# A weight stream placed between the steps of a serial chain by a table, and split in half chunks

## The chip, the cores and the metric

The kernel runs on one core of a Trainium2 chip. The metric is the device time of one execution in microseconds (us), the median of the timed runs. The engines are TensorE (PE), VectorE (DVE), ScalarE (ACT), GpSimd (POOL) and SyncE (SP), each with its own queue of instructions that it works through in order. They wait for each other with semaphores only.

## The reference, cut to what matters

Two decoder layers are computed for 256 prompt tokens and 8 sample tokens together, T = 264 columns with D_MODEL = 2048. All in float32:

```python
# per layer
h = x @ w_in                                   # 2048 x 19024, columns shared out among five branches
# A gated delta rule (chunked, triangular solve)    B sparse attention: indexer, top-k, gather, softmax
# C retention (chunkwise recurrent)                 D RG-LRU: conv, gates, linear scan
# E cross-attention into 256 memory tokens (w_mem_kv)
merged = sum(sigmoid(gate_b) * (y_b @ w_branch[b]) for b in branches)
out = merged @ w_out                           # 2048 x 2048
x = layer_norm(ALPHA * x + out)
...
s = jnp.einsum('bqhd,bsd->bqhs', qi_blk, ki_all).astype(jnp.float32)      # indexer
score = jnp.einsum('bqhs,bqh->bqs', jax.nn.relu(s), w_blk.astype(jnp.float32))
_, idx = lax.top_k(score, ksel)                # 256 of 2049 keys for each sample, 64 of 256 in the prompt
...
m = jnp.eye(c) + jnp.where(strict, beta[..., :, None] * kk * decay, 0.0)  # delta rule
sol = lax.linalg.triangular_solve(m, rhs, left_side=True, lower=True, unit_diagonal=True)
```

## The kernel before, in words

Two kinds of work share the engines. The **weight stream** is dense: each layer has 174 chunks of 128 output columns and the whole contraction (2048 rows, KC = 16 K steps). For each chunk SP loads 1 MB into one of two `ring` buffers (L520). ACT rounds it to the high part of a split in fp32r (L1022), DVE subtracts to get the low part (L1267), each into one of two `wsplit` buffers, and PE does three matmuls for each K step (high x high, high x low, low x high, L564 to L566) with the activations `xsplit`, into a bank of `mb`. The 8 chunks of w_mem_kv are not split (L554, L557). ACT evacuates a chunk (`stored`, or the sigmoid of a gate). A chunk of a gate has four more matmuls behind it, the branch projection (L575), each two instructions in float32, and DVE multiplies and adds into `merged` (L1295, L1297, L1298).

The **chain** is everything else: a long series of small steps, each of which needs the one before. PE does a few small matmuls or transposes into `bb`, DVE or ACT works on the result, PE goes on. In order of the program: memory attention (`attend(0)`, `sample_attend(0)`), small gates, the lightning indexer over 8 page groups (L738, L743, L747), three convolutions (L1531), norms, the triangular inverse (two tiles of six levels, L843, L847, L848), the delta rule's output, its state steps for samples (`samples_step`, L881, L889), retention with its own, RG-LRU, rotations, copies of rows to the outputs, prompt indexer, sparse attention, gather and `sample_attend(1)`. The top-k of the samples is 32 rounds of four DVE instructions on a row of 2049 scores (`topk`, L1313 to L1316), strewn over the chain from the inverse on. The state tiles, the keys and the values for samples come by POOL's DMA queue.

The order of all work is written out by hand. In the code of each engine `stream(n)` stands between chain steps and issues that engine's part of the next n chunks, whole chunks only. On ACT and DVE `ahead()` and `stream` also issue the split of the coming chunk (`split_to`). PE runs its `stream` behind the chain matmul whose answer it will wait for. Behind the last chain step `stream(None)` issues what is left. A branch's gates may only be streamed once its output is done.

The numbers behind the letters: a K step is three matmuls, a branch step one float32 matmul, a layer has 2784 K steps and 320 branch steps. The lines of the small functions named here are below.

## Time and profile before

| | |
|---|---|
| median of three runs | 3554.73 us (3553.57 to 3561.67) |
| profiled execution, first to last instruction | 3562.9 us |
| TensorE busy | 3125.1 us, 88% |
| VectorE busy | 2040.6 us, 57% |
| ScalarE busy | 940.3 us, 26% |
| mean granted TensorE clock | 0.913 |
| DMA | 485.89 MB, mean 136 GB/s |

The spans of matmuls overlap, since they are pipelined, so a sum of their lengths is more than PE's busy time. Idle time counts only on the engine that the others wait for. The granted clock is 1.00 at 2.4 GHz and 0.50 at 1.2 GHz; a mean between them says how long either held.

### The profile page before, as it was taken

What the parts mean: (1) busy time and instruction counts of PE and PEld (TensorE: products, weight loads), DVE (VectorE), ACT (ScalarE), POOL (GpSimd) and SP (SyncE); (2) the same over time, 40 slices, a digit from 0 to 9 for tenths busy, and PEclk for the clock granted to TensorE, in tenths of its full rate; (3) what the DMA queues carried; (4) which work ended last, traced back from release to release, by engine and by line L of the source; (5) the groups of instructions that cost most, each with busy time, mean ns of one, the idle gap of its engine ahead of it and who ended that gap; (6) DMA issues with size and microseconds to landing.
All of it is one profiled execution on the core that took longest, in us unless ns stands there. A gap on an engine that the chain in (4) does not pass through costs nothing. (4 is left out here: it accounts for less than half of the span.)

```text
span 3562.9 us, 50279 instructions
## 1 busy us (share of the span) xinstructions
PE 3125.1 (88%) x21476; PEld 2907.0 (82%) x21476; DVE 2040.6 (57%) x2274; ACT 940.3 (26%) x969; POOL 186.2 (5%) x206
## 2 busy tenths in 40 slices
PE   6998887898888999999779988888978879999995
PEld 5888787887777898999778887788878778989995
DVE  2153267769868776344413532766798697653444
ACT  2232132212133232223313222322121422322232
POOL 0000000000000002100000000000000000031000
PEclk9988898998889999999989888999898999999998
DMA  5664343353544556665356632433535445675651
GB/s 154 166 173 129 101 121 83 104 142 107 148 116 107 161 148 192 169 175 157 83 139 174 189 103 87 121 103 108 138 101 143 128 126 139 163 197 164 177 157 60
DMA packets 825220, 485.89 MB, mean 136 GB/s; under 512 B 20548, under 2 KB 807108, under 8 KB 823746
## 3 DMA queue, kind: packets, MB, share of 16 engines
q1 hardware_dynamic: 803760, 409.93, 43.3%
q0 software_dynamic: 19936, 66.89, 6.1%
q10 hardware_dynamic: 1296, 5.80, 0.4%
q8 instruction: 172, 2.82, 0.3%
q14 instruction: 56, 0.46, 0.0%
HBM read 466.22 MB, written 16.47 MB: 135 GB/s over the span
## 5 line engine op out<-in xcount | busy, mean ns | idle before, releaser
L564 PE MATMUL mb<-xsplit,wsplit 128*128 128x264 f32 (+1 forms) x5312 | 1615.1, 304 | 164.4 <-DVE wsplit L1267 150.9
L565 PE MATMUL mb<-xsplit,wsplit 128*128 128x264 f32 (+1 forms) x5312 | 1569.1, 295 | 0.0
L566 PE MATMUL mb<-xsplit,wsplit 128*128 128x264 f32 (+1 forms) x5312 | 1564.8, 295 | 0.0
L564 PEld LDWEIGHTS mb<-xsplit,wsplit 128*128 128x128 f32 (+1 forms) x5312 | 1066.5, 201 | 215.0 <-DVE wsplit L1267 168.4
L565 PEld LDWEIGHTS mb<-xsplit,wsplit 128*128 128x128 f32 (+1 forms) x5312 | 1065.6, 201 | 4.3
L566 PEld LDWEIGHTS mb<-xsplit,wsplit 128*128 128x128 f32 (+1 forms) x5312 | 1057.1, 199 | 1.1
L1267 DVE TENSOR_TENSOR wsplit<-ring,wsplit 128x2048 fp32r<-128x2048 f32 x332 | 753.1, 2269 | 338.2 <-ACT wsplit L1022 324.8
L1022 ACT ACTIVATE wsplit<-ring 128x2048 fp32r<-128x2048 f32 x332 | 627.8, 1891 | 165.6 <-PE mb L566 109.7
L1049 ACT ACTIVATE gbuf<-mb 128x264 f32<-128x264 f32 x160 | 62.6, 391 | 1024.2 <-PE mb L566 967.3
L575 PE MATMUL mb<-work,bring 128*128 128x264 f32 x1280 | 310.6, 385 | 0.0
L1297 DVE TENSOR_TENSOR gbuf<-gbuf,mb 128x264 f32<-128x264 f32 x128 | 54.8, 428 | 422.6 <-PE mb L575 420.3
L1063 ACT ACTIVATE work<-mb 128x264 f32<-128x264 f32 x136 | 52.9, 389 | 810.8 <-PE mb L566 810.8
L575 PEld LDWEIGHTS mb<-work,bring 128*128 128x128 f32 x1280 | 231.3, 189 | 31.6
L1313 DVE MAX8 m<-memkv 8x8 f32<-8x2049 f32 x64 | 145.7, 2277 | 0.1
L1314 DVE FIND_INDEX8 i<-m,memkv 8x8 uint32<-8x2049 f32 x64 | 145.6, 2275 | 0.0
L1315 DVE MATCH_REPLACE8 memkv<-m,memkv 8x2049 f32<-8x2049 f32 x64 | 145.1, 2267 | 0.0
L1489 DVE SCALAR_TENSOR_TENSOR work<-bb,scm 128x1024 f32<-128x1024 f32 x16 | 19.6, 1225 | 163.5 <-PE bb L743 163.5
L675 PEld LDWEIGHTS bb<-small,work 128*128 128x128 f32 x512 | 72.2, 227 | 11.5 <-DMA work<-in_cache_mem_v_dram 10.9
L675 PE MATMUL bb<-small,work 128*128 128x1 f32 x512 | 71.6, 274 | 10.6 <-DMA work<-in_cache_mem_v_dram 10.6
L889 PE MATMUL bb<-work 8*128 8x512 f32 x64 | 44.2, 823 | 31.6 <-DVE work L1650 31.6
L847 PE MATMUL bb<-work 128*128 128x128 f32 x192 | 47.9, 338 | 16.5 <-ACT work L1174 16.5
L747 PEld LDWEIGHTS bb<-tab,work 128*128 128x128 f32 x256 | 31.1, 199 | 34.3 <-DVE work L1489 34.3
(392 smaller groups left out, 2437.5 us busy)
## 6 DMA issues: line engine op xcount, KB each, us to landing
ring<-in_w_in_dram SPq DMA_DIRECT2D x296, 1024.0 KB, 5.8
bring<-in_w_branch_dram SPq DMA_DIRECT2D x160, 256.0 KB, 3.2
ring<-in_w_out_dram SPq DMA_DIRECT2D x32, 1024.0 KB, 6.0
ring<-in_w_mem_kv_dram SPq DMA_DIRECT2D x16, 1024.0 KB, 5.5
work<-in_cache_mem_k_dram POOLq DMA_DIRECT2D x16, 512.0 KB, 4.1
work<-in_cache_mem_v_dram POOLq DMA_DIRECT2D x16, 512.0 KB, 4.1
work<-in_mem_prompt_dram ACTq DMA_DIRECT2D x2, 2048.0 KB, 12.2
work<-in_state_gdn_dram POOLq DMA_DIRECT2D x8, 512.0 KB, 5.1
```

Of the source, the lines that this page charges most:

```text
L564: pe.matmul(bank[0:n, 0:T], wh, ah, start=first, stop=False)
L565: pe.matmul(bank[0:n, 0:T], wh, al, start=False, stop=False)
L566: mm = pe.matmul(bank[0:n, 0:T], wl, ah, start=False, stop=last)
L575: mm = pe.matmul(mb[:, (g + 1) % 4, 0:T], bring[:, j % 2, q, :], y[:, q, :], start=(q == 0), stop=(q == CPS - 1))
L675: mm = pe.matmul(bb[:, 0, j:j + 1], kvb[:, b % 2, t, h * P:(h + 1) * P], pts[:, 32 * t + j:32 * t + j + 1], start=(t == 0), stop=(t == 1))
L1022: act.activation(hi(wsplit[:, s % 2, 0, :, 0:n]), ring[:, j % NRING, :, 0:n], ACT.Copy)\
L1049: act.activation(gbuf[:, :], src[:, 0:T], ACT.Sigmoid).then_inc(sem.gate_act, 1)
L1267: dve.tensor_tensor(hi(wsplit[:, s % 2, 1, :, 0:n]), ring[:, j % NRING, :, 0:n], wsplit[:, s % 2, 0, :, 0:n], ALU.subtract).then_inc(sem.l ...
L1297: v(dve.tensor_tensor(gbuf[:, :], gbuf[:, :], proj, ALU.mult))
L1313: v(dve.max(m8[:, :], srow))
L1314: v(dve.max_index(i8[:, :], m8[:, :], srow))
L1315: v(dve.match_replace(srow, m8[:, :], srow, TAKEN))
```

## The change

The stream is issued in steps instead of chunks. `STEP` lists all K steps and branch steps of a layer in order. The table `PACE` gives each chain step's name and how many steps PE runs behind it (`fill`). ACT and DVE have `before(name)` and `upto(pos)`: they issue all splits and evacuations that are due at a position of the stream. Chunks, their order and the chain's order stay. The load, the high part and the low part of a chunk are made in two halves of 8 K steps, with four half buffers in `ring` and in `wsplit`, so the bytes held are the same. A buffer of `wsplit` comes free after half a chunk (`half_mm`). DVE's part of a split is due four steps behind ACT's. Top-k rounds are cut by stream work at a third and two thirds of the fill they are named after. Splitting `merged` for w_out begins during the last gate (`merged_hi`, `merged_lo`). A semaphore without a reader, `lc_ok`, is gone.

```diff
-NRING = 2
+NRING = 4
...
+HALF = KC // 2
+for _i, (_k, _, _) in enumerate(CHUNKS):
+    START.append(len(STEP))
+    STEP.extend((_i, q) for q in range(KC + CPS * (_k == "gate")))
+def half_done(s):
+    return START[SPLIT[s // 2]] + HALF * (1 + s % 2)
+def hi_due(s):
+    i = SPLIT[s // 2]
+    read = done(i - 2) if i >= 2 and CHUNKS[i - 2][0] == "mem" else 0
+    return max(read, half_done(s - 4) if s >= 4 else 0)
+def lo_due(s):
+    return hi_due(s) + 4 * (s >= 4)
...
+PACE = """
...
+    gc 13  tail0 26  tail1 27  tail2 25  conv 24  ss1 19  norm1 6  ss2 25  tok0 12  kk 6  invT0 5  invA0 12  y00 3
...
-        ring = sb("ring", [P, NRING, KC, P])
-        wsplit = sb("wsplit", [P, 2, 2, KC, P])
+        ring = sb("ring", [P, NRING, HALF, P])
+        wsplit = sb("wsplit", [P, 4, 2, HALF, P])
...
+                        for half in range(2):
+                            r = 2 * i + half
+                            if i >= 2:
+                                if CHUNKS[i - 2][0] == "mem":
+                                    sp.wait_ge(sem.chunk_mm, products(i - 2))
+                                else:
+                                    sp.wait_ge(sem.lo_ok, 2 * SPLIT_N[i - 2] + half + 1)
+                            sp.dma_start(ring[:, r % NRING, :, 0:n], w[:, half * HALF:(half + 1) * HALF, c0:c0 + n])\
+                                .then_inc(w_landed[r % NRING], 16)
...
+                    def stream(n):
+                        for i, q in STEP[at[0]:at[0] + n]:
+                            if q < KC:
+                                weight_step(i, q)
+                            else:
+                                branch_step(i, q - KC)
+                        at[0] += n
+                    def fill(name):
+                        stream(FILL[name])
...
-                            stream(2)
+                            fill(f"lg{n}{t}")
...
+                    def upto(pos):
+                        while True:
+                            s, i = nxt_half[0], nxt_chunk[0]
+                            a = hi_due(s) if s < 2 * len(SPLIT) else pos + 1
+                            b = (START[i] if CHUNKS[i][0] == "out" else START[i] + KC) if i < len(CHUNKS) else pos + 1
+                            if min(a, b) > pos:
+                                return
+                            if a <= b:
+                                split_half(s)
+                                nxt_half[0] += 1
+                            else:
+                                evacuate(i)
+                                nxt_chunk[0] += 1
...
+                    def merged_hi(q):
+                        act.wait_ge(sem.merged_ok, LAST * KC + 4 * q + 4)
...
                             v(dve.max(m8[:, :], srow))
+                            upto(AT[name] + FILL[name] // 3)
                             v(dve.max_index(i8[:, :], m8[:, :], srow))
+                            upto(AT[name] + 2 * FILL[name] // 3)
                             v(dve.match_replace(srow, m8[:, :], srow, TAKEN))
                             v(dve.tensor_copy(picked[:, 8 * r:8 * r + 8], i8[:, :]))
+                            upto(AT[name] + FILL[name])
```

Three places show how instructions move. First DVE at the start of the delta rule's sample states: `COPY work<-bb 128x32` takes up PE's product of keys and queries, L1313 to L1316 are a top-k round, L1267 a split, L1295 a gate's finish. Before:

```order
L1625 COPY work<-bb 128x32 [waits qk_mm]
L1626 COPY work<-bb 8x512 [waits v_chain]
L1267 TENSOR_TENSOR wsplit<-ring,wsplit 128x2048 [waits hi_ok]
L1313 MAX m<-memkv 8x8
L1314 MAX_INDEX i<-m,memkv 8x8 [waits v_chain]
L1315 MATCH_REPLACE memkv<-m,memkv 8x2049 [waits v_chain]
L1316 COPY scm<-i 8x8 [waits v_chain]
L1295 TENSOR_TENSOR merged<-gbuf,mb 128x264 [waits chunk_mm,gate_act,v_chain]
```

In the changed kernel (L1389 to L1394 is the round, L1328 half a split, L1351 the gate's finish):

```order
L1701 COPY work<-bb 128x32 [waits qk_mm,v_chain]
L1702 COPY work<-bb 8x512 [waits v_chain]
L1389 MAX m<-memkv 8x8
L1391 MAX_INDEX i<-m,memkv 8x8 [waits v_chain]
L1328 TENSOR_TENSOR wsplit<-ring,wsplit 128x1024 [waits hi_ok,v_chain]
L1393 MATCH_REPLACE memkv<-m,memkv 8x2049
L1394 COPY scm<-i 8x8 [waits v_chain]
L1328 TENSOR_TENSOR wsplit<-ring,wsplit 128x1024 [waits hi_ok,v_chain]
L1351 TENSOR_TENSOR merged<-gbuf,mb 128x264 [waits chunk_mm,gate_act]
```

The split stood ahead of the round as one piece; its work is now two halves inside and behind the round.

Second DVE at the end of the RG-LRU, where L1727 is the product with the gate path and L1730 the copy that PE waits for. Before, from the second of two rounds on:

```order
L1313 MAX m<-memkv 8x8 [waits v_chain]
L1314 MAX_INDEX i<-m,memkv 8x8 [waits v_chain]
L1315 MATCH_REPLACE memkv<-m,memkv 8x2049 [waits v_chain]
L1316 COPY scm<-i 8x8 [waits v_chain]
L1297 TENSOR_TENSOR gbuf<-gbuf,mb 128x264 [waits chunk_mm,gate_act,v_chain]
L1298 TENSOR_TENSOR merged<-merged,gbuf 128x264 [waits v_chain]
L1267 TENSOR_TENSOR wsplit<-ring,wsplit 128x2048 [waits hi_ok]
L1297 TENSOR_TENSOR gbuf<-gbuf,mb 128x264 [waits chunk_mm,gate_act]
L1298 TENSOR_TENSOR merged<-merged,gbuf 128x264 [waits v_chain]
L1727 TENSOR_TENSOR work<-work 128x1056 [waits stored,lru_o]
L1730 COPY stg<-bb 9x512 [waits tail_out,h_mm,v_chain]
```

After, from the end of the first round on (L1795 and L1799 are that product and that copy):

```order
L1393 MATCH_REPLACE memkv<-m,memkv 8x2049
L1394 COPY scm<-i 8x8 [waits v_chain]
L1328 TENSOR_TENSOR wsplit<-ring,wsplit 128x1024 [waits hi_ok,v_chain]
L1328 TENSOR_TENSOR wsplit<-ring,wsplit 128x1024 [waits hi_ok]
L1353 TENSOR_TENSOR gbuf<-gbuf,mb 128x264 [waits chunk_mm,gate_act]
L1354 TENSOR_TENSOR merged<-merged,gbuf 128x264 [waits v_chain]
L1389 MAX m<-memkv 8x8
L1391 MAX_INDEX i<-m,memkv 8x8 [waits v_chain]
L1393 MATCH_REPLACE memkv<-m,memkv 8x2049 [waits v_chain]
L1394 COPY scm<-i 8x8 [waits v_chain]
L1795 TENSOR_TENSOR work<-work 128x1056 [waits stored,lru_o,v_chain]
L1799 COPY stg<-bb 9x512 [waits tail_out,h_mm,v_chain]
```

The splits and gates that stood behind the second round now all stand inside and behind the first, and the second is bare.

Third PE in the triangular inverse, between the first level's products (L847, L848) and the next level (L843). Before:

```order
L848 MATMUL bb<-work 128x128
L843 MATMUL bb<-work 128x128 [waits lvl_bt]
L843 MATMUL bb<-work 128x128 x3
L847 MATMUL bb<-work 128x128 [waits y_ok]
L848 MATMUL bb<-work 128x128
L847 MATMUL bb<-work 128x128
```

After, at the first level (L921 is the level's first product, L606 to L608 a K step, L625 a branch step, L926 and L927 the level's other products):

```order
L921 MATMUL bb<-work 128x128 [waits lvl_bt]
L921 MATMUL bb<-work 128x128 x3
L625 MATMUL mb<-work,bring 128x264 x2
L606 MATMUL mb<-xsplit,wsplit 128x264 [waits lo_ok,stored]
L607 MATMUL mb<-xsplit,wsplit 128x264
L608 MATMUL mb<-xsplit,wsplit 128x264
L926 MATMUL bb<-work 128x128 [waits y_ok]
L927 MATMUL bb<-work 128x128
```

Where no stream work stood there are now two branch steps and a K step at the wait for `y_ok`, and the table puts eight more behind the level's last product.

## Rows read from the trace of the kernel before

**Rows 1.** The cores view, and the engines' busy shares from the page.
```profile
core 0: 3562.9 us, clock 0.913
...
PE 3125.1 (88%) x21476; PEld 2907.0 (82%) x21476; DVE 2040.6 (57%) x2274; ACT 940.3 (26%) x969; POOL 186.2 (5%) x206
```

**Rows 2.** Windows of layer 1's chain, one of layer 2's; columns in the first line.
```profile
core 0: us, PE busy (x) PEld busy (x) DVE busy (x) ACT busy (x) POOL busy (x), PEclk, DMA share, GB/s
145.00:344.80 199.80, 181.26 (x1243) 168.34 (x1242) 92.94 (x103) 62.13 (x75) 15.43 (x21) 0.86 0.60 168
344.80:476.70 131.90, 113.66 (x680) 99.68 (x679) 34.06 (x36) 30.35 (x29) 8.05 (x7) 0.83 0.31 90
476.70:567.70 91.00, 74.05 (x551) 71.10 (x549) 68.99 (x109) 32.85 (x31) 3.61 (x7) 0.94 0.51 133
567.70:753.20 185.50, 164.54 (x1153) 156.73 (x1154) 120.51 (x124) 38.51 (x41) 3.14 (x4) 0.93 0.38 100
753.20:1022.20 269.00, 227.15 (x1414) 202.52 (x1412) 232.53 (x216) 56.42 (x52) 14.69 (x17) 0.84 0.48 129
1022.20:1261.80 239.60, 204.54 (x1414) 191.33 (x1413) 184.10 (x221) 74.96 (x77) 7.02 (x13) 0.94 0.48 130
1261.80:1477.10 215.30, 209.13 (x1462) 193.19 (x1460) 124.22 (x153) 63.26 (x71) 41.17 (x32) 0.96 0.65 180
1477.10:1745.50 268.40, 263.16 (x2002) 256.71 (x2001) 116.46 (x106) 79.10 (x62) 0.00 (x0) 0.99 0.59 157
1799.80:3235.00 1435.20, 1274.81 (x8627) 1178.81 (x8628) 871.64 (x974) 370.41 (x390) 92.84 (x101) 0.90 0.50 136
850.00:900.00 50.00, 36.47 (x230) 33.55 (x229) 49.24 (x38) 9.97 (x9) 0.00 (x0) 0.84 0.26 67
```

**Rows 3.** Windows with the stream alone: gates, then w_out.
```profile
1500.00:1550.00 50.00, 50.00 (x369) 48.16 (x368) 22.99 (x24) 15.34 (x14) 0.00 (x0) 1.00 0.65 174
1655.00:1745.00 90.00, 90.00 (x745) 90.00 (x745) 40.28 (x30) 26.89 (x14) 0.00 (x0) 1.00 0.56 152
```

**Rows 4.** Lines of the whole run: count, busy us, mean ns, idle before.
```profile
L1313 DVE MAX8 m<-memkv 8x8 f32<-8x2049 f32 x64 | 145.7, 2277 | 0.1
L1315 DVE MATCH_REPLACE8 memkv<-m,memkv 8x2049 f32<-8x2049 f32 x64 | 145.1, 2267 | 0.0
L1297 DVE TENSOR_TENSOR gbuf<-gbuf,mb 128x264 f32<-128x264 f32 x128 | 54.8, 428 | 422.6 <-PE mb L575 420.3 <-ACT gbuf L1049 1.5
```

**Rows 5.** Waits of the whole run: us in total, times, longest us.
```profile
PE mb L564 <- DVE wsplit L1267: 150.9, 54, 36.4
...
PE bb L747 <- DVE work L1489: 21.1, 16, 1.3
```

**Rows 6.** Lines: VectorE in 753.2 to 1022.2, then ScalarE in the whole run.
```profile
L1267 DVE TENSOR_TENSOR wsplit<-ring,wsplit 128x2048 fp32r<-128x2048 f32 x23 | 52.6, 2286 | 0.3
...
L1647 DVE TENSOR_TENSOR work<-work,tab 128x1024 f32<-128x1024 f32 x4 | 4.9, 1225 | 0.1
...
L1129 ACT ACTIVATE work<-bb 128x1024 f32<-128x1024 f32 x16 | 16.4, 1024 | 63.1 <-PE bb L738 63.1
```

**Rows 7.** DMA issues of the whole run: KB each, median us to landing.
```profile
ring<-in_w_in_dram SPq DMA_DIRECT2D x296, 1024.0 KB, 5.8
...
work<-in_cache_mem_k_dram POOLq DMA_DIRECT2D x16, 512.0 KB, 4.1
```

**Rows 8.** Timeline at the start of layer 2: start us, length us.
```profile
1788.76 11.56 SPq L520 DMA_DIRECT2D ring<-in_w_in_dram  x3
...
1795.55 1.91 ACT L1022 ACTIVATE wsplit<-ring 128x2048 fp32r<-128x2048 f32 x1 [5.43 <-DMA ring<-in_w_in_dram]
1798.83 1.91 ACT L1022 ACTIVATE wsplit<-ring 128x2048 fp32r<-128x2048 f32 x1 [1.37 <-DMA ring<-in_w_in_dram]
...
1797.49 2.29 DVE L1267 TENSOR_TENSOR wsplit<-ring,wsplit 128x2048 fp32r<-128x2048 f32 x1 [18.53 <-ACT wsplit L1022]
...
1799.84 0.59 PE L564 MATMUL mb<-xsplit,wsplit 128*128 128x264 f32 x1 [36.35 <-DVE wsplit L1267]
```

More of the change, by code:

```diff
@@ L132, in kv_count @@
+"""
+FILL, AT = {}, {}
+for _name, _n in zip(PACE.split()[::2], PACE.split()[1::2]):
+    AT[_name] = sum(FILL.values())
+    FILL[_name] = int(_n)
 def kv_count(n, i):
@@ L717, in _ @@
                     mm.then_inc(sem.ki_mm, 1)
-                    stream(1)
+                    fill("ki")
                     for c in range(CPS):
@@ L731, in _ @@
                     mm.then_inc(sem.new_mm, 1)
-                    stream(1)
+                    fill("new")
                     for j in range(8):
@@ L772, in tail @@
                         mm.then_inc(sem.tails, 1)
+                        fill(f"tail{i}")
                     def ones_sum(n, src):
@@ L1270, in _, with split_half @@
-                    at_chunk = [0]
-                    def ahead():
-                        split_to(at_chunk[0] + 1)
-                    def stream(n=1):
-                        for i in islice(chunks, n):
-                            (kind, x, m), g = CHUNKS[i], FIRST_RESULT[i]
-                            if kind == "gate" and x == LAST and m < 4:
+                    nxt_half, nxt_chunk = [0], [0]
+                    def split_half(s):
+                        i = SPLIT[s // 2]
+                        r = 2 * i + s % 2
+                        n = COL_NARROW[CHUNKS[i][2]][1] if CHUNKS[i][0] == "narrow" else P
+                        dve.wait_ge(sem.hi_ok, s + 1)
+                        dve.tensor_tensor(hi(wsplit[:, s % 4, 1, :, 0:n]), ring[:, r % NRING, :, 0:n],
+                                          wsplit[:, s % 4, 0, :, 0:n], ALU.subtract).then_inc(sem.lo_ok, 1)
@@ L1738, in _ @@
                     for j in range(7):
+                        before(f"row{j}")
                         dve.wait_ge(sem.rows_mm, 3 + j)
-                        ahead()
                         if j and j not in (4,):
```

635 lines of the change are left out of this document (314 added, 321 removed).

## The prediction

> **What bounds the kernel now.** I read span, clock and busy shares first [rows 1]: one program of 3562.9 us, about 8 us above the 3554.73 us median of the timed runs. TensorE (PE) is what the rest serves, since the weight stream runs through it from end to end. So I cut the span into stretches of layer 1 and read busy time and granted clock in each [rows 2]. The cuts are the starts of chain stages: 145.0 memory attention, 344.8 indexer, 476.7 convolutions and norms, 567.7 triangular inverse and delta rule, 753.2 sample states and retention, 1022.2 RG-LRU and row copies, 1261.8 sparse attention, 1477.1 stream alone until 1745.5. Layer 2 (from 1799.8) shows the same picture: 160.4 us idle and clock 0.90 in its chain part.
>
> A stretch loses PE time in two ways. Its idle time is its length less PE's busy time. Its clock loss is busy time times (1 less the granted clock), since the two levels are 2.4 and 1.2 GHz. In order of the stretches (idle + clock, us): 18.5+25.4, 18.2+19.3, 17.0+4.4, 21.0+11.5, 41.9+36.3, 35.1+12.3, 6.2+8.4, 5.2+2.6. That is 163 idle and 120 clock, 283 us of 1600.5.
>
> Third, where the stream runs dense, what does it cost? 745 recorded matmuls fill 90.0 us at full clock [rows 3], 0.121 us each, so a K step of three costs 0.36 us. In the stretch of gates alone 369 matmuls take 50 us, 56 to a gate: 7.6 us a gate, of which 5.8 are its 16 K steps and 1.8 its four branch steps, 0.44 each.
>
> Fourth, is VectorE (DVE) a second bound? It is busy 232.5 of 269.0 us in the stretch from 753.2, and 49.2 of 50.0 us in 850 to 900, where PE falls to 36.5 [rows 2]. A top-k round is three passes of 2.27 to 2.28 us, 6.8 us [rows 4], and a split is 2.29 [rows 6]. There the chain waits for DVE, not for PE. Last, the waits [rows 5]: the split is PE's largest releaser (150.9 us, 36.4 of it at a layer's start), and the others are many short ones, as the indexer's 16 waits of at most 1.3 us.
>
> **The change part by part.**
>
> *The stream spread over the waits.* Nothing is computed less. PE now runs whole chunks (5.8 us, a gate 7.6) at some waits and none at others, as the third block of order rows shows: no weight matmul between two levels of the inverse. After it every wait gets its own number of steps. I counted steps in both programs between the same chain steps. Per stretch, after less before (K steps, branch steps): +6/0, +1/0, +10/0, -29/-4, +110/+12, -6/+12, -77/-20, -15/0. They sum to nothing. At 0.36 and 0.44 us these are +2.2, +0.4, +3.6, -12.2, +44.9, +3.2, -36.6, -5.4 us. The full-clock floor of PE is the stretch less its loss plus this: 158.1, 94.8, 73.2, 140.8, 235.7, 195.4, 164.1, 255.2 us.
>
> *DVE's load moves with it.* The 110 steps taken into the stretch from 753.2 bring 6.9 more chunks at 2.29 = 15.7 us of splits [rows 6], and three more gate finishes, each one operation of 0.43 in the first branch's gates, 1.3 us [rows 4]. So stream goes to the place where DVE is fullest, away from 1261.8, where it has 124 of 215 us.
>
> *Splits in halves.* A DVE operation on 1024 columns from SBUF takes 1225 ns, one on 2048 columns 2286 in the same stretch [rows 4, 6]. Two halves cost 2450, so 0.16 us more per chunk, on DVE 332 x 0.16 = 54 us in all. It lies beside PE except where DVE leads: 479 steps or 30 chunks from 753.2, 4.8 us. ScalarE (ACT) has 1.91 us for a whole chunk [rows 8], and 1.02 for 1024 columns out of PSUM [rows 6]; if the half costs 1.0 to 1.1, two cost 0.1 to 0.3 more, hidden since ACT is busy at most 75 of 240 us in a stretch. DVE needs in the stretch from 753.2: 232.5+15.7+1.3+4.8 = 254.3 us. At the 98% that DVE reaches in 850 to 900 this is 259 us, at its present 86% it is 294. That is above PE's 235.7: DVE sets this stretch. In the stretch from 1022.2 (6 K steps fewer, three gates of two such operations more, 23.5 chunks in halves) it is 184.1-0.9+2.6+3.8 = 189.6 against PE's 195.4, in the one from 476.7 it is 72.1 against 73.2: neither hides the other.
>
> *Loads in halves, four buffers.* The same bytes are in flight. A 1024 KB load lands in 5.8 us, 512 KB in 4.1 [rows 7]. At a layer's start [rows 8] the load is issued at 1788.76, ACT starts at 1795.55, DVE at 1797.49, PE at 1799.84. With halves the landing comes 1.7 us earlier (5.8-4.1), ACT's part is 0.8 to 0.9 shorter and DVE's 1.1: 3.6 us, and about 4.5 if the first landing there gains more, since it took 6.8. I take 4.5, twice: 9 us. A buffer comes free every 2.9 us in the dense part, and each has 11.6 us for landing, both splits and its matmuls, so the loads hold.
>
> *The tail of the last gates.* The split of merged is started before the last gate is done. It is inside the 5.2 us of idle time of the last stretch; its end is counted below.
>
> *What stays of the losses.* No row shows a wait with a fill made for it. The lower end is that nothing stays: the floors, with 259 in place of 235.7, give 1341 us a layer, 259.5 saved, and 3562.9-519-9 = 3035. The upper end is that all stays as it is: with DVE at its present share the stretches from 753.2, 476.7 and 1022.2 grow with its work by 25.2, 4.1 and 7.2 us, the others change by their moved steps (-51.6), so 15.1 us a layer are saved and it is 3524. I take the middle, half of either loss: the waits that now get a fill were bare or half covered, but the clock falls also in stretches with hardly a gap, and top-k rounds of 6.8 us stand against fills of 15 to 17 steps (5.4 to 6.1). Stretches: 180.1, 113.5, 83.9, 157.1, 275 (DVE at 93%, between its two shares), 219.1, 171.4, 259.1: 1459.2 us, 141.3 saved a layer. In all 3562.9-282.6-9 = 3271 us as a profiled execution, 3263 beside the median.
>
> *Where the new order costs.* At the end of the RG-LRU (second block of order rows) the first of two top-k rounds is now cut up by all splits of a 71-step fill, and the second follows bare, before the copy that PE waits for. PE's fill is 55 K and 16 branch steps, 26.8 us. DVE has 10 halves (12.3), four gate finishes (3.4), two rounds (13.7) and 1.3 for the product before the copy: 30.7. PE waits some 4 us there per layer. Behind that copy PE has the rotations queued, and POOL its two stores. It is part of the half that stays.
>
> *The clock.* In the indexer PE's waits for DVE are 1.3 us at most [rows 5], and yet the granted clock is 0.83 with PE busy 113.7 of 131.9 us; from 476.7 to 567.7, with almost the same idle time in fewer us, it is 0.94 [rows 2]. The Trainium skill (TensorE: Matmul & The Clock Gate, "HAM oscillation — how this bites in real kernels") has it that long PE idle gaps bring the clock down, and that a kernel without them stays warm. By that rule all clock loss would go and the time would be some 120 us lower than my sum; the trace of the indexer does not agree, and so half of it stays.
>
> **The rivals.**
>
> *The clock stays as low.* The chain's narrow matmuls are all still there, and the indexer's row speaks for it. Then half of the clock loss outside the stretch that DVE sets, 42 us a layer, is not gained: 3263+84 = 3347 us.
>
> *Nearly everything is recovered.* The stretch 1500 to 1550 shows PE at 50.00 of 50.00 and clock 1.00 with the stream alone. If the fills reach that and a fifth of the loss stays, 3035+0.2x489 less 8 = 3125 us. Against it stand the top-k rounds above.
>
> *DVE is the bound all over.* Its share stays at today's in each stretch, and the spread only shifts PE's waits: the upper end, 3516 beside the median.
>
> *Half loads pay their fixed part one after another.* From [rows 7] 2x4.1-5.8 = 2.4 us. A chunk would take 8.2 us to load against 5.8 in the 16 chunks of w_out and 7.6 in 21 gates: 38+13 = 51 us a layer, 3263+102 = 3365. Against it: two whole loads in a row were split 3.3 us apart [rows 8], so loads overlap. The Trainium skill (DMA: Bandwidth & Descriptors, "Anatomy of one DMA — SWDGE (gpsimd) path") gives a fixed part of about 2.0 us per DMA, close to these 2.4; the rule speaks against the change only if nothing overlaps.
>
> *Slower: the top-k rounds get in the chain's way.* After the change a round is cut at a third and at two thirds of a fill and ends only when the splits due within that fill are done, which wait for PE's position. DVE can no longer run ahead of PE, and the chain's next DVE operation, with PE behind it, comes late. There are 32 rounds a layer. If three in four cost their 6.8 us on the path, 24x6.8 = 163 us a layer are given back, and it is 3263+326 = 3589 us. It decides from 21 rounds on (146 us). For it: the block at the end of the RG-LRU. Against it: most fills are about as long as DVE's work beside them.
>
> **How the numbers follow.** The forecast, half of the losses gone, 3265 us: 0.45, own range 3190 to 3330. Clock as low: 0.19. Nearly everything: 0.16. Half loads in a row: 0.05. DVE bound all over: 0.08. Slower: 0.07. The range of 8 in 10 is 3140 to 3420: it leaves out DVE all over, the slower case, and the tip of the low one. 0.3%, or 11 us, is what a measurement of this kernel tells from no change. Faster takes the first four and three quarters of DVE all over, since that end is itself uncertain by more than 11 us: 0.91. Same 0.02, slower 0.07.
>
> **What would show it right or wrong.** PE's busy share rises from 88% to 92 to 94%, and the mean granted clock from 0.913 to about 0.95. The stretch of sample states and retention stays near 270 us with DVE above 90% busy, the one of sparse attention falls from 215 to about 171, the indexer's from 132 to about 113. 664 splits of about 1.2 us stand on DVE and of 1.0 to 1.1 on ACT. The first matmul of layer 2 comes 4 to 5 us sooner after the first load is issued. Wrong would be: a clock below 0.92 with idle time halved (the first rival), ring loads above 6 us with ACT waiting for them in the dense part (the fourth), or PE waits for DVE behind top-k passes that sum to more than now (the last). The forecast falls if the stretch from 753.2 takes more than 300 us, or if sum of idle time in the chain part stays above 120 us a layer.

## The result, and the profile after

The changed kernel takes 3137.06 us, the median of four runs (3134.06 to 3142.06), against 3555.2 us (3553.57 to 3561.67) for the kernel before: ratio 0.8821, 95% interval 0.8809 to 0.8834. The direction was right. The forecast of 3265 us was 128 us too slow, and the time lies 3 us below the low end of the range. The case that came true is the second rival, nearly everything is recovered (3125 us), which had a chance of 0.16.

The cores view and the page's busy shares of the kernel after answer to [rows 1]. PE's busy time fell by 199 us although it issues the same 21476 matmuls; the clock losses summed below (120 us a layer before, 22 after) account for it:

```profile
core 0: 3135.3 us, clock 0.973
```

```profile
PE 2926.4 (93%) x21476; PEld 2747.5 (88%) x21476; DVE 2072.8 (66%) x2606; ACT 1005.7 (32%) x1303; POOL 170.1 (5%) x206
```

The windows view, cut at the same chain steps as in [rows 2], in the same order, with layer 2 as the last row:

```profile
core 0: us, PE busy (x) PEld busy (x) DVE busy (x) ACT busy (x) POOL busy (x), PEclk, DMA share, GB/s
138.20:304.00 165.80, 162.01 (x1265) 151.95 (x1265) 95.70 (x121) 67.51 (x99) 15.42 (x21) 1.00 0.72 207
304.00:395.30 91.30, 91.30 (x683) 83.41 (x682) 34.68 (x45) 28.93 (x34) 6.30 (x7) 1.00 0.47 134
395.30:477.80 82.50, 74.58 (x581) 72.09 (x579) 70.81 (x120) 35.70 (x45) 3.75 (x7) 0.98 0.54 149
477.80:624.00 146.20, 142.81 (x1098) 136.92 (x1099) 121.00 (x138) 39.16 (x52) 3.13 (x4) 1.00 0.44 122
624.00:889.40 265.40, 243.70 (x1729) 225.34 (x1728) 249.00 (x255) 80.48 (x97) 14.68 (x17) 0.95 0.56 156
889.40:1103.50 214.10, 199.09 (x1417) 187.31 (x1416) 188.92 (x262) 76.71 (x97) 7.05 (x13) 0.97 0.53 148
1103.50:1267.80 164.30, 163.99 (x1174) 150.44 (x1172) 105.26 (x143) 54.91 (x77) 34.71 (x32) 1.00 0.70 194
1267.80:1528.60 260.80, 258.33 (x1974) 252.01 (x1975) 121.69 (x143) 85.42 (x97) 0.00 (x0) 0.99 0.57 158
1578.00:2809.00 1231.00, 1176.60 (x8606) 1099.36 (x8606) 884.41 (x1104) 398.68 (x522) 84.88 (x101) 0.98 0.57 160
```

A stretch's length less PE's busy time, the two numbers behind the range, is its idle time; the clock stands behind POOL's numbers. The indexer's row is the plainest: 131.9 us with PE busy 113.66 at clock 0.83 [rows 2] has become 91.3 us, PE busy all of it, at 1.00. In sum layer 1's chain and stream take 1390.4 us, 210 less than before. Of the 163 us of idle time a layer 55 are left, of the 120 us of clock loss 22 (busy time times 1 less the clock, summed over the eight rows). The largest part of the one and more than half of the other, 21.7 and 12.2 us, are in the one row from 624.0, where DVE is busy 249.0 of 265.4 us.

The waits view of the kernel after (us in total, times, longest) answers to [rows 5]. The wait for the split is 59 us smaller, and 46 of its 91.5 us are the starts of the two layers (32.6 at the second, the longest; 13.5 by the same view of the first 304 us). The 21.1 us of the indexer's sixteen waits have no row any more. L778, the wait behind the end of the RG-LRU, is the largest inside the chain:

```profile
PE mb L606 <- DVE wsplit L1328: 91.5, 30, 32.6
...
PE bb L778 <- DVE stg L1799: 17.7, 2, 8.8
...
PE mb L606 <- DVE work L1618: 9.4, 2, 4.7
PE bb L970 <- DVE work L1726: 7.3, 6, 1.8
```

The lines of the split, by form (count, busy us, mean ns), answer to [rows 6]:

```profile
L1328 DVE TENSOR_TENSOR wsplit<-ring,wsplit 128x1024 fp32r<-128x1024 f32 x656 | 794.8, 1222 | 651.0 <-ACT wsplit L1108 641.5 <-issue 3.3
...
L1108 ACT ACTIVATE wsplit<-ring 128x1024 fp32r<-128x1024 f32 x656 | 692.4, 1058 | 1593.3 <-PE mb L608 1451.2 <-DMA ring<-in_w_in_dram 102.3 <-issue 39.0
```

And the timeline at the start of layer 2 answers to [rows 8]. From the load's issue to PE's first matmul it is now 7.07 us, 4.0 less than the 11.08 before. ACT starts on the first two half loads 1.81 us apart:

```profile
1573.10 7.55 SPq L561 DMA_DIRECT2D ring<-in_w_in_dram  x5
1577.80 1.06 ACT L1108 ACTIVATE wsplit<-ring 128x1024 fp32r<-128x1024 f32 x1 [3.44 <-DMA ring<-in_w_in_dram]
1578.89 1.23 DVE L1328 TENSOR_TENSOR wsplit<-ring,wsplit 128x1024 fp32r<-128x1024 f32 x1 [15.89 <-ACT wsplit L1108]
1579.61 1.06 ACT L1108 ACTIVATE wsplit<-ring 128x1024 fp32r<-128x1024 f32 x1 [0.75 <-DMA ring<-in_w_in_dram]
...
1580.17 0.59 PE L606 MATMUL mb<-xsplit,wsplit 128*128 128x264 f32 x1 [32.65 <-DVE wsplit L1328]
```

### The profile page after: what moved, and what is told of

Read it like the earlier page. It is cut to its first block and busy times, and to the rows that moved or that the text cites. A ratio compares the mean times of both kernels' runs of the same rounds, so it can differ in the third digit from the quotient of the medians.

```text
span 3135.3 us, 52446 instructions
## 1 busy us (share of the span) xinstructions
PE 2926.4 (93%) x21476; PEld 2747.5 (88%) x21476; DVE 2072.8 (66%) x2606; ACT 1005.7 (32%) x1303; POOL 170.1 (5%) x206
## 5 line engine op out<-in xcount | busy, mean ns | idle before, releaser
L606 PE MATMUL mb<-xsplit,wsplit 128*128 128x264 f32 (+1 forms) x5312 | 1589.6, 299 | 110.2 <-DVE wsplit L1328 91.5
L607 PE MATMUL mb<-xsplit,wsplit 128*128 128x264 f32 (+1 forms) x5312 | 1518.3, 286 | 0.0
L608 PE MATMUL mb<-xsplit,wsplit 128*128 128x264 f32 (+1 forms) x5312 | 1516.8, 286 | 0.0
L1328 DVE TENSOR_TENSOR wsplit<-ring,wsplit 128x1024 fp32r<-128x1024 f32 (+2 forms) x664 | 798.7, 1213 | 661.6 <-ACT wsplit L1108 651.9
L1108 ACT ACTIVATE wsplit<-ring 128x1024 fp32r<-128x1024 f32 (+2 forms) x664 | 696.2, 1051 | 1608.0 <-PE mb L608 1458.3
L606 PEld LDWEIGHTS mb<-xsplit,wsplit 128*128 128x128 f32 (+1 forms) x5312 | 1008.8, 190 | 169.3 <-DVE wsplit L1328 74.9
L607 PEld LDWEIGHTS mb<-xsplit,wsplit 128*128 128x128 f32 (+1 forms) x5312 | 1009.6, 190 | 10.5 <-issue 3.8
L608 PEld LDWEIGHTS mb<-xsplit,wsplit 128*128 128x128 f32 (+1 forms) x5312 | 1004.7, 189 | 1.1
L625 PE MATMUL mb<-work,bring 128*128 128x264 f32 x1280 | 318.7, 390 | 0.0
L625 PEld LDWEIGHTS mb<-work,bring 128*128 128x128 f32 x1280 | 232.9, 192 | 33.4 <-issue 1.5
L1389 DVE MAX8 m<-memkv 8x8 f32<-8x2049 f32 x64 | 145.6, 2275 | 0.0
L744 PE MATMUL bb<-small,work 128*128 128x1 f32 x512 | 58.9, 245 | 0.0
L1354 DVE TENSOR_TENSOR merged<-merged,gbuf 128x264 f32<-128x264 f32 x128 | 55.4, 433 | 4.4
L595 PE MATMUL mb<-ring,work 128*128 128x128 f32 x512 | 57.8, 275 | 0.0
L595 PEld LDWEIGHTS mb<-ring,work 128*128 128x128 f32 x512 | 57.6, 192 | 0.1
L592 PE MATMUL mb<-work,ring 128*128 128x256 f32 x256 | 55.6, 379 | 0.0
L592 PEld LDWEIGHTS mb<-work,ring 128*128 128x128 f32 x256 | 48.5, 190 | 6.5
## 6 DMA issues: line engine op xcount, KB each, us to landing
work<-in_mem_prompt_dram ACTq DMA_DIRECT2D x2, 2048.0 KB, 11.8
```

The costliest lines, as they stand in the source:

```text
L592: mm = pe.matmul(bank[:, 0:NMEM], w, memT[:, q, :], start=first, stop=last)
L595: mm = pe.matmul(bank[:, t * P:(t + 1) * P], memT[:, q, t * P:(t + 1) * P], w, start=(first and t == 0), stop=last, skip_group_check=True)
L606: pe.matmul(bank[0:n, 0:T], wh, ah, start=first, stop=False)
L607: pe.matmul(bank[0:n, 0:T], wh, al, start=False, stop=False)
L608: mm = pe.matmul(bank[0:n, 0:T], wl, ah, start=False, stop=last)
L625: mm = pe.matmul(mb[:, (g + 1) % 4, 0:T], bring[:, j % 2, q, :], y[:, q, :], start=(q == 0), stop=(q == CPS - 1))
```

## Experiments: which part of the change is worth what

All are edits of the changed kernel. The ratios are to the kernel before, which took 3560 to 3561 us beside the experiments and 3555.2 us beside the changed kernel. A difference in microseconds between an experiment and the changed kernel is therefore uncertain by some 5 us.

### Old places, halves kept

The table alone is changed: PACE gives every wait what stood behind it before, in whole chunks of 16 or 20 steps.

```diff
-    lead 64  param 16  memT0 2  memT1 2 ... lg00 24  pT00 8  ov00 6 ...
-    ... ikT0 4  ikm0 8  iks0 3  ikT1 5  ikm1 9  iks1 3 ...
+    lead 64  param 16  memT0 0  memT1 0 ... lg00 32  pT00 16  ov00 16 ...
+    ... ikT0 16  ikm0 0  iks0 0  ikT1 16  ikm1 0  iks1 0 ...
```

> The changed kernel with another table: every chain step gets the stream that the kernel before had there, in whole chunks (a fill ends at a chunk's end). Halves, four buffers, the early split of merged and the position-driven queues stay. Theory A, the placement alone took the clock loss and the idle time: about 3540 us, before less some 10 to 20 us for layer starts and the tail. Rival B, half buffers are what lets DVE and ACT keep up: at least half of the 418 us stays gained, below 3350 us. Rival C, the queues cut by position cost something: above 3560 us.

Measured: 3475.37 us (3472.46 to 3482.72), ratio 0.9772 (0.9756 to 0.9789). What is left of the change without its places brings 80 to 85 us, more than theory A gave it and much less than B. That is the halves together with the early split of `merged` and the queues that go by position, neither of which was tried by itself. PE's wait for the split is 73.5 us against 150.9 before [rows 5], which is 77 of these 80 to 85 us and speaks for the halves. The other waits of this run show that the old picture is back, down to the 16 waits of the indexer with the same 21.1 us as in [rows 5] (L821 here), at a mean clock of 0.918:

```profile
PE mb L606 <- DVE wsplit L1328: 73.5, 8, 32.6
PE bb L970 <- DVE work L1726: 48.3, 16, 5.4
PE bb L921 <- DVE work L1665: 27.6, 8, 4.9
...
PE bb L821 <- DVE work L1568: 21.1, 16, 1.3
```

### Whole chunks, table kept

```diff
-NRING = 4
+NRING = 2
-        ring = sb("ring", [P, NRING, HALF, P])
-        wsplit = sb("wsplit", [P, 4, 2, HALF, P])
+        ring = sb("ring", [P, NRING, KC, P])
+        wsplit = sb("wsplit", [P, 2, 2, KC, P])
```

Load, high part and low part are whole again, and due when a whole buffer comes free.

> The changed kernel with its table, but loads and splits in whole chunks and two buffers each, as before the change. Theory A: little is lost, at most some 30 us (3140 to 3170): 4.5 us at either layer start and the chain's waits behind a split of 2.29 us in place of 1.23. Rival B: the table needs the halves, since a buffer comes free only at a chunk's end and DVE's split then falls late: above 3250 us, seen as PE waits for the split.

Measured: 3261.42 us (3250.85 to 3268.58), ratio 0.9171 (0.9156 to 0.9186). Theory A falls, and rival B comes out, both by the time and by the wait: with fine fills the halves are worth 124 us, not the 33 at most that theory A expected. PE now waits 202 us for the split, 110 more than in the changed kernel:

```profile
PE mb L604 <- DVE wsplit L1324: 201.7, 62, 36.2
```

The four corners as ratios to before are 1, 0.977 without the new places, 0.917 without the halves, 0.882 with both. The two in the middle save 2.3 and 8.3 points, the whole 11.8: at least 1.2 points, some 43 us, come only from having both (at least, since the early split of `merged` and the queues by position are counted in both of the middle ones).

### Whole loads, half splits

```diff
-                        for half in range(2):
-                            r = 2 * i + half
...
-                            sp.dma_start(ring[:, r % NRING, :, 0:n], w[:, half * HALF:(half + 1) * HALF, c0:c0 + n])\
+                        sp.dma_start(ring[:, i % NRING, :, 0:n], w[:, :, c0:c0 + n]).then_inc(w_landed[i % NRING], 16)
```

> The changed kernel (table and half splits), but with loads of whole chunks (1 MB) into two buffers, each freed when its second half is split. It tells which half of the halving matters. Theory A (the splits in halves bring the 124 us that e2 lacked, since a half buffer of the split comes free 2.9 us sooner; the loads are never late in the dense part): 3140 to 3150 us, of which 2 x 1.7 us are the later first landing of each layer. Rival B (the loads' finer grain matters, since a whole load can only start when the whole buffer before it is split, and lands 5.8 us later): 3180 to 3250 us, with ScalarE waiting for ring loads.

Measured: 3177.76 us (3175.89 to 3181.09), ratio 0.892 (0.8906 to 0.8934), 41 us slower than the changed kernel. Theory A is wrong by 28 us. Rival B's 3180 us is nearly met, and ScalarE does wait for the loads, but the time is lost at the layers' starts only. The windows below, of the changed kernel and of this one, reach to the start of the indexer: 25 us are lost there. From there to the last row copy of layer 1 it is 754.8 against 753.9 us, and then again 25.3 us are lost up to the indexer of layer 2 (some 7 us come back later in layer 2).

```profile
0.00:304.00 304.00, 273.22 (x2031) 252.20 (x2032) 122.99 (x169) 92.47 (x142) 15.63 (x25) 1.00 0.64 182
```

```profile
0.00:329.20 329.20, 282.87 (x2031) 261.11 (x2032) 122.08 (x169) 91.31 (x142) 15.63 (x25) 0.96 0.59 167
```

Of the 25.2 us, 15.5 are idle time of PE and 9.7 longer busy time, at a clock of 0.96 in place of 1.00. The stream begins 2.4 us later, its first four chunks' 192 matmuls take 31.4 us in place of 25.4, and where the split resumes behind the eight unsplit chunks PE runs 97 matmuls in 18.3 in place of 14.5 us. Two chain steps of VectorE make PE wait 4.8 and 2.7 us more; the rest is not traced. ScalarE's wait for loads in the whole run, of the changed kernel and then with whole loads:

```profile
ACT wsplit L1108 <- DMA ring<-in_w_in_dram: 109.9, 48, 10.8
...
ACT wsplit L1105 <- DMA ring<-in_w_in_dram: 526.8, 109, 12.7
```

So of the 124 us a third is due to half loads, at the layers' starts, and by subtraction two thirds (83 us) to half splits with their buffers that come free sooner. In mid-layer the later landing is covered: there ScalarE's longer wait costs nothing, as the 754.8 against 753.9 us show.

### Positions in steps of eight

Every position of the table is rounded to the nearest multiple of eight steps, by a fill's sum.

```diff
-    ... ikT0 4  ikm0 8  iks0 3  ikT1 5  ikm1 9  iks1 3  ikT2 5  ikm2 8 ...
+    (cumulative position p of each name) -> 8 * round(p / 8)
```

> The changed kernel with every position of the table rounded to the nearest multiple of 8 steps (half a chunk, 2.9 us of PE). A fill changes by at most 8 steps, the stages' totals by at most 8. Theory A (each wait needs its own small fill, because what is left bare costs idle time and the clock with it): the indexer's fills of 3 to 5 steps become 0 or 8, so about a third of the 170 waits a layer lose their cover; at about 1 us a bare wait this is 30 to 60 us a layer with the clock's share, 3137 + 60 to 120: 3200 to 3255 us. Rival B (it was enough to get away from whole chunks; a layer's waits even out): 3137 to 3160 us.

Measured: 3214.74 us (3212.64 to 3216.83), ratio 0.9029 (0.9016 to 0.9043). Theory A: 78 us of the table's gain need fills finer than eight steps. The indexer's stretch is 100.9 us, PE 7.1 of it idle:

```profile
307.50:408.40 100.90, 93.80 (x679) 84.38 (x678) 33.73 (x44) 30.02 (x36) 6.33 (x7) 0.98 0.44 121
```

## Experiments: idle time and the clock

### All fills of an indexer round in its first wait

```diff
-    ikT0 4  ikm0 8  iks0 3  ikT1 5  ikm1 9  iks1 3 ...
+    ikT0 15  ikm0 0  iks0 0  ikT1 17  ikm1 0  iks1 0 ...
```

> Of the eight rounds of the indexer only: the 15 to 18 steps of each round all stand at its first wait (behind the transposes), none at the other two. Theory, the clock falls where narrow matmuls and short waits stand together: the stretch 304.0 to 395.3 us of layer 1 grows from 91.3 to about 118, with a granted clock near 0.85 as before the change, and the kernel to about 3190 us. Rival, only idle time counts and the clock needs long gaps: the stretch grows by its bare waits alone, 8 x 2.2 = 18 us at clock 1.00, no slow stretch in it, 3173 us.

Measured: 3198.16 us, ratio 0.8991 (0.8976 to 0.9006), 8 us above the theory's total, and in the stretch both its numbers come out (118 us and 0.85 expected, 120.5 and 0.87 measured); the rival falls. The windows row over the whole stretch, to the first convolution, and the two waits in it:

```profile
304.20:424.70 120.50, 107.83 (x682) 95.97 (x681) 35.23 (x45) 29.31 (x34) 6.34 (x7) 0.87 0.37 102
```

```profile
PE bb L821 <- DVE work L1568: 10.5, 8, 1.3
PE bb L811 <- DVE scm L1572: 1.9, 7, 0.3
```

Against the changed kernel's 91.3 us at 1.00 this is 29.2 us more: 12.7 of idle time and, at the same work, 16.5 of longer busy time. Fifteen waits of at most 1.3 us thus cost more through the clock than by themselves. By windows of a microsecond, the clock falls in the second round shortly before 328 us (0.92 from 327 to 328 us, 0.50 in the next one). That is amid the sixteen two-column matmuls behind the 1.3 us wait, where PE is busy all the time. The following lump starts at the lower level, and the timeline shows the return. The three matmuls of a K step begin 0.22 us apart at the lower level and 0.12 apart at the higher:

```profile
333.98 0.42 PE L607 MATMUL mb<-xsplit,wsplit 128*128 128x264 f32 x1
334.20 0.42 PE L608 MATMUL mb<-xsplit,wsplit 128*128 128x264 f32 x1
...
335.03 0.28 PE L607 MATMUL mb<-xsplit,wsplit 128*128 128x264 f32 x1
335.15 0.28 PE L608 MATMUL mb<-xsplit,wsplit 128*128 128x264 f32 x1
```

### Narrow matmuls in the bare waits

Float32 matmuls of two columns whose results nothing uses are added. The 20 behind the products stand in the first bare wait. The 14 stand behind the transposes' fill, a wait that the lump covers already, and the second bare wait (0.3 us) stays bare: not quite what the expectation says.

```diff
                         mm.then_inc(sem.ik_T, 1)
                         fill(f"ikT{j}")
+                        narrow(2, 14)
...
                         mm.then_inc(sem.ik_mm, 1)
                         fill(f"ikm{j}")
+                        narrow(1, 20)
```

> As the lumps in the indexer, but PE's two bare waits of each round are filled with matmuls of 2 columns (14 and 20 of them, results unused), so that PE is hardly idle there. If idle time is what lowers the clock: clock back to 1.00 in this stretch. If narrow matmuls count as little work: clock as low as with the lumps alone, 0.85 or lower, and the stretch about as long or up to 10 us longer.

Measured: 3370.37 us, ratio 0.9473 (0.9457 to 0.9488). The whole stretch:

```profile
306.00:516.00 210.00, 207.86 (x1226) 193.86 (x1225) 35.20 (x45) 29.27 (x34) 6.34 (x7) 0.72 0.21 59
```

The longest waits in it are of 0.3 us:

```profile
PE bb L816 <- DVE scm L1579: 1.9, 7, 0.3
PE bb L834 <- DVE scm L1579: 0.3, 1, 0.3
```

PE is busy 99% and the clock is 0.72, lower than with the waits bare, so the absence of idle time doesn't hold the clock here. The expected length is missed by far: 210 us in place of about 120 to 130. Each added matmul is two instructions (1226 recorded for 682), and 20 of them take 4.9 us in one round and 8.5 in another, against a bare wait of 1.3. So the run shows what long narrow work does, and not what a fill of the wait's own length would do.

### Wide matmuls in the bare waits

The lumps again, with matmuls of the stream's kind in the two bare waits: ten and two of 264 columns, results unused.

```diff
+                            pe.matmul(bb[:, bank, 0:T], hi(xsplit[:, 0, 0, 0:P]), hi(xsplit[:, 0, 0, :]), start=True, stop=True)
...
+                        wide(1, 10)
                         fill(f"ikm{j}")
...
+                        wide(1, 2)
                         fill(f"iks{j}")
```

> As e3 (all fills of an indexer round in its first wait, the two others bare), but with wide matmuls whose results nothing uses in the bare waits: ten of 264 columns in the first and two in the second, of the kind that the stream is made of. They are 96 a layer, 96 x 0.121 = 11.6 us of PE work at full clock on top of the 95.3 x 0.89 = 84.8 us that e3 has there. Theory A (the clock falls with bare waits, and comes back with wide work in them): granted clock 0.98 or more, the indexer's stretch about 97 to 100 us against 107.7 in e3, the whole 3175 to 3185 us against 3198, in spite of the added work. Rival B (the clock there is set by the chain's narrow matmuls themselves, and not by the waits): clock stays 0.89, the stretch takes 96.4 / 0.89 = 108 to 112 us, the whole 3200 to 3210 us.

Measured: 3186.35 us (3182.36 to 3191.22), ratio 0.895 (0.8937 to 0.8964), 12 us faster than without the added work. The row, over the whole stretch (the 107.7 and 95.3 us quoted above were of a window that ended within the last round; the whole is the 120.5 and 107.83 of the lumps alone):

```profile
304.35:418.70 114.35, 113.49 (x779) 102.99 (x778) 35.22 (x45) 29.19 (x34) 6.35 (x7) 0.93 0.39 108
```

At full clock the work is 113.49 x 0.93 = 105.5 us against 107.83 x 0.87 = 93.8, so 11.7 more, as added, and the stretch still takes 6.1 us less. Neither number comes out: the clock is neither 1.00 nor 0.87. Wide work in the waits gives back about half of the clock loss, and the rest stays with almost no idle time. Here the chain's own parts still follow each other closely, as the timeline of one round shows (L809 are the added ones), and then comes the lump; in the changed kernel 2 to 10 K steps lie between any two of them.

```profile
349.44 1.88 PE L821 MATMUL bb<-work,Qblk 128*128 128x512 f32 x4
350.76 1.77 PE L809 MATMUL bb<-xsplit 128*128 128x264 f32 x10
352.64 1.95 PE L827 MATMUL bb<-tab,work 128*128 128x2 f32 x16
354.44 0.49 PE L809 MATMUL bb<-xsplit 128*128 128x264 f32 x2
354.85 1.72 PE L816 MATMUL bb<-tab,work 128*128 128x128 f32 x8
```

That this spreading is what brings the other half is the likeliest reading, and no run separates it. With positions in steps of eight, where some of these parts follow each other and 7.1 us are idle, the clock is 0.98.

## Experiments: VectorE's work and the top-k rounds

### Totals of two stretches as before

110 steps are taken from the fills kq0 to yc in proportion and given to those from row0 on.

```diff
-    qk0 21  sk00 19  vt00 10  op00 7 ...   (kq0 to yc: 542 steps; row0 to sy1: 540)
+    the same fills x 432/542, and x 650/540
```

> The changed kernel, but 110 steps a layer taken out of the stretch of sample states and retention and given to the one from the row copies through sparse attention, each spread in proportion over that stretch's fills. That is the share that the two stretches had before. Theory A (PE's spare time in the states was wasted before, and the 110 steps fill it): the stretch of states, which VectorE sets (249 us busy of 265.4), gets VectorE's 17 us less and falls to about 248; the other grows by the 110 steps at 0.36 us, from 164.3 to about 203. Net 20 us a layer worse, 3175 us. Rival B (only the fineness counts, the totals hardly do, since VectorE gets free as fast as PE gets loaded): the states' stretch falls by the full 110 x 0.36 = 40 us, 3137 to 3145 us.

Measured: 3195.88 us (3193.11 to 3197.72), ratio 0.8972 (0.8958 to 0.8986). Theory A: the move of 110 steps is worth 59 us, 29 a layer against 20 expected. The windows from the first sample step's transpose to the fourth convolution, of the changed kernel, then of this one:

```profile
637.50:903.30 265.80, 244.52 (x1736) 226.42 (x1737) 248.19 (x246) 83.69 (x99) 14.68 (x17) 0.96 0.55 154
```

```profile
641.40:894.10 252.70, 218.59 (x1444) 198.87 (x1445) 231.87 (x228) 68.53 (x82) 14.68 (x17) 0.90 0.48 132
```

With 110 steps less the stretch falls by 13.1 us only and DVE's share is 92% against 93%: DVE sets it, as reckoned. PE's clock falls to 0.90 as it goes without work.

### Rounds not cut by splits

```diff
                             v(dve.max(m8[:, :], srow))
-                            upto(AT[name] + FILL[name] // 3)
                             v(dve.max_index(i8[:, :], m8[:, :], srow))
-                            upto(AT[name] + 2 * FILL[name] // 3)
                             v(dve.match_replace(srow, m8[:, :], srow, TAKEN))
```

> The changed kernel, but a top-k round is not cut by splits at a third and two thirds of its fill: its passes of 2.27 us each run one after another and the splits that are due come behind them. Theory A (splits are what PE needs next, so a split that comes 6.8 us late makes PE wait): with 25 rounds a layer that lie in fills and a half buffer's slack of 2.9 to 5.8 us, about 1 to 2 us a round are lost, 3137 + 50 to 100, 3190 to 3235 us. Rival B (the cuts get in the chain's way, as my slower case had it): uncut rounds are faster, 3110 us or less. If the ring's slack of four half buffers holds, nothing changes.

Measured: 3191.63 us (3186.62 to 3196.31), ratio 0.8962 (0.8948 to 0.8976). Theory A: 55 us slower, and 45 us of it stand in one row, PE's wait for the split (91.5 us in the changed kernel):

```profile
PE mb L606 <- DVE wsplit L1328: 136.3, 29, 32.6
```

### One round moved from the end of the RG-LRU

```diff
-                    topk("h", 2)
+                    topk("h")
-    ... h 71 ... topk 61 ...
+    ... h 55 ... topk 77 ...
```

> The changed kernel, but the second, bare top-k round at the end of the RG-LRU is left to the block of rounds before the gather, with 16 steps of the fill (71 to 55 there, 61 to 77 here). Theory A (VectorE's queue of 30.7 us against PE's 26.8 is what makes the wait of 8.8 us before the copy of h, and there is no other reason): the wait falls under 2 us, VectorE has room later, 3137 - 12 to 17: 3120 to 3125 us. Rival B (the round costs its 6.8 us wherever it stands, since the last rounds before the gather are bare for PE too): 3135 to 3140 us.

Measured: 3129.91 us (3128.77 to 3135.36), ratio 0.8793 (0.8781 to 0.8805). The wait of 8.8 us is gone (L778 now waits 1.8 us a layer, for another line), but only 7 us are gained of 17.7 (10 by the ratios). From layer 1's fourth convolution to the last row copy it takes 143.8 us in place of 154.6, where the moved steps are 5.8 of the difference; behind it 5.8 us come with them and some 3 of new idle time. Both theories are half right.

### Two more rounds to where VectorE has time

```diff
-                    topk("ss3")
-                    topk("tok1")
...
+                            if n and t:
+                                topk(f"lg{n}{t}")
```

On top of the edit before; the last block's two rounds are spread over its fill.

> e8 with two more top-k rounds (of ss3 and tok1) taken out of the stretch of states and retention, which VectorE sets, one put between the exponential's request and its answer in sparse attention (lg11) and the other into the block before the gather, whose two rounds are now spread evenly over its fill. PE's steps stay where they are. Theory A (VectorE's rounds in the states are on the path, and VectorE has 18 us without work in sparse attention): 13.6 us less on VectorE in the stretch, PE idle there falls by 8 to 12 us a layer, the whole 3130 - 15 to 25: 3105 to 3115 us. Rival B (what VectorE does in the states is followed by waits on PE anyway): 3125 to 3135 us.

Measured: 3129.43 us (3124.57 to 3132.99), ratio 0.8786 (0.8774 to 0.8798), the same as the edit before. Rival B by the number, but not by its reason: the fourth convolution starts at 891.1 in place of 903.4, 12 us earlier, and this row is new:

```profile
PE bb L694 <- DVE work L1440: 15.8, 2, 7.9
```

The round ahead of the softmax's normalisation had PE waiting 7.9 us a layer.

### The same, the round behind the output step

```diff
-                            if n and t:
-                                topk(f"lg{n}{t}")
...
+                            if n and not t:
+                                topk(f"ov{n}{t}")
```

> e10, but the round that stood in lg11, ahead of the softmax's normalisation, where PE waited 7.9 us a layer for it, stands behind the first tile's output step (ov10), where the trace of e8 shows VectorE without work for some 6 us and PE with 17 and then 32 steps to run. Theory A (e10 saved 12 us a layer in the stretch of states, as the start of the fourth convolution at 891.1 against 903.4 us shows, and gave them back in that one wait): the wait falls under 2 us a layer, 3129 - 12 to 16: 3113 to 3118 us. Rival B (VectorE's slack in sparse attention is not there, the time comes back in other waits): 3125 to 3130 us.

Measured: 3119.52 us (3114.9 to 3121.09), ratio 0.876 (0.8748 to 0.8772). This beats both kernels, by 17.5 us the changed one. The wait of 7.9 us a layer is gone, but PE now waits 3.8 us for the attention's output step on VectorE (second block; 1.5 us in the run with one round moved), where under 2 us were expected. The median lies 1.5 us above the expected 3113 to 3118, less than the runs differ:

```profile
core 0: 3113.2 us, clock 0.976
```

```profile
PE mb L606 <- DVE work L1447: 7.6, 2, 3.8
```

```profile
639.20:893.20 254.00, 242.19 (x1736) 223.73 (x1737) 234.15 (x234) 84.17 (x99) 14.71 (x17) 0.97 0.60 161
```

The stretch of states is 11.8 us shorter than in the changed kernel, with DVE's work 14.0 us less.

## Why the prediction was right and wrong

*What bounded the kernel* was right: PE's idle time and clock in the chain, and DVE from the sample states on.

*Stream spread over the waits.* The floors were about right. Sparse attention reached its floor (164.3 us for 164.1), the indexer went below it (91.3 for 94.8), and the inverse came within 6 (146.2 for 140.8).

*The step that failed is "half of either loss stays".* It added up to 1459.2 us a layer and 1390.4 were measured. Of idle time I kept 81 us, 55 stayed; of clock loss 60, 22 stayed. These two, 27 and 38, are 65 of the 69 us a layer, 130 of the 136 us by which the profiled execution beat my 3271. The clock is the larger part. The idle time was kept for the top-k rounds, which I set whole against the fills. Cut by splits they hold up less: uncut, PE waits 45 us more for the split, and with whole splits 110 us more. My reason for keeping half of it was the indexer, where the clock was low with waits of 1.3 us at most. I read that as a sign that the clock would stay low whatever filled the waits. The runs contradict that reading: the loss came from those waits together with the unbroken narrow matmuls around them, and how much from either stays open. With lumps the clock is 0.87 there, with fills between all parts 1.00, and wide work alone in the waits gives 0.93. The Trainium skill (TensorE: Matmul & The Clock Gate, "HAM oscillation — how this bites in real kernels") says that long idle gaps bring the clock down. By that rule all clock loss had to go, which was closer to the result than my half. The start of layer 2 agrees: behind 32.65 us of idle time the matmuls begin 0.22 us apart. The indexer does not: lumps fell to 0.87 with no wait over 1.3 us, and narrow matmuls to 0.72 with no wait over 0.3 us in that stretch.

*The first rival* (clock stays low, 3347) fell by the same rows, and *DVE the bound all over* (3516) too: only one stretch is set by DVE. There the sum was good. Forecast 275 us with DVE at 93%; measured 265.4 with DVE at 94%, because its work is 249.0 and not the reckoned 254.3.

*Half loads in a row* (3365) fell: ACT starts on the first two half loads of layer 2 1.81 us apart, and the experiment with whole loads is 41 us slower, so halving them is a gain. The price behind this rival, the 4.1 us of [rows 7], was of a load by POOL's queue, and the section quoted beside it is on that path too, while the ring loads go by SP's queue. The profile after gives no landing time for them. The forecast gave the loads only the 9 us of the two first landings, of which 8 came. It missed that a layer's first chunks and the ones behind the unsplit chunks run no deeper than the buffers: 25 us a layer.

*Splits in halves* cost 1222 ns in place of 1225 each and 1058 in place of 1000 to 1100, as forecast. That they cost DVE 0.16 us a chunk more was right and beside the point. I gave them no gain at all in the stream, and the runs show 83 us, by subtraction. My reading is that a buffer that comes free after half a chunk lets ACT and DVE be ahead of small fills, which PE's wait of 201.7 us for whole splits, against 91.5 for halves, bears out.

*Slower by the top-k rounds* (3589) fell, and by a wide margin in the other direction: uncut rounds are 55 us slower. I priced only what the cut delays, not what an uncut round of 6.8 us delays, the next split. (146 us a layer are 22 such rounds, not 21.)

*End of the RG-LRU.* The wait was put at 4 us a layer and is 8.8. Queue against queue was the wrong sum. DVE's work beside the fill goes at PE's pace, since each split waits for a buffer, and DVE was idle about 5 us in it. It ended the last gate at 979.2 us, when PE's fill was all but over, and the bare second round (7.2), the product (1.3) and the copy (0.7) were still to come. All of them were waited for.

The range left out the case that came true by 3 us. It went down to 3140 with that case's time at 3125 and a chance of 0.16, so it left out more than the tip of that case. The cases that it held in full have chances of 0.69 together, not eight in ten: the low end should have reached further.

## What to carry to other kernels

Where PE's clock is low in a stretch of many short waits between narrow matmuls, count the clock loss as gained when each wait gets wide work of its own size (1.00 in the indexer here), and count most of it as kept when the same work is put in one lump (0.87). A placement and the grain of the buffers that feed it are one change: fine fills need splits that come free at the same grain. When a slow step of a full engine has to be moved, look for its slack behind the last answer that another engine waits for and not ahead of it.

## What the runs showed of the hardware

- TensorE busy is not TensorE at speed. With 99% busy the granted clock in the indexer was 0.72 when two-column float32 matmuls were added and 0.93 with 264-column ones. With the waits bare it was 0.87 at 89% busy, and with stream work between all parts 1.00.
- Useless wide work can pay: 11.7 us of it made the indexer's stretch 6.1 us shorter, 114.35 for 120.5.
- Two halves of a VectorE subtraction of 2048 columns cost 2 x 1222 ns against 2286 whole, 7% more.
